# The last four steps' expert results summed on chip, and a place of its own for the first expert's w1 in the second layer

## Chip, cores and metric

The kernel runs on one core of one Trainium2 chip. The metric is the device time of one execution in microseconds; three executions of the kernel before took 1209.22 to 1213.81 us, median 1212.03. All data are fp32.

## What is computed

Two layers over 256 image rows (x) and 256 context rows (ctx) of 1024 columns. Each layer: modulation, one input projection cut into five groups (Fourier mix, differential attention, gated unit), output projection, residual and layer norm. Then comes the part that matters here, a mixture of 16 experts of which each row uses 2:

```python
def _moe(h, gates, w1, w3, w2):
    y = jnp.zeros_like(h)
    for e in range(N_EXPERTS):                       # 16
        a = jax.nn.silu(h @ w1[e]) * (h @ w3[e])     # 1024 -> 512
        y = y + gates[..., e:e + 1].astype(h.dtype) * (a @ w2[e])
    return y

    hx = _modulate(x, sh2, sc2)
    yx = _moe(hx, _route(hx, w_router, router_bias), moe_w1[l], moe_w3[l], moe_w2[l])
    x = _layernorm(DEEPNORM_ALPHA * x + g2 * yx, ln_g[l, 1], ln_b[l, 1])
    # ctx likewise, in the first layer only
```

`_route` gives each row two experts with weights that sum to 1. The experts' three matrices are 2 MB each, 6 MB an expert, 96 MB a layer.

## The kernel before

It is written engine by engine, with semaphores; each engine runs its own program in order. Rows stand in tiles of 128: T = 4 tiles in layer 0 (2 of x, 2 of ctx), T = 2 in layer 1. PSUM has 8 banks; `plan_layer` hands them out job by job (`claim`, `full`, `freed`, `read`), and an `("at", b)` skips to bank b.

**Experts as steps.** Rows are sorted by expert into blocks of 32 (`ROWS`). Each block is a step; an expert has one step or more, and their number is known only at run time (`META`, written by DVE after routing: counts, steps before each expert, steps in all). The trace shows 41 steps in layer 0, five of them the first expert's, and 25 in layer 1, one of them the first expert's. Per step: PE `turn_rows` (transposes), `up` (w1 and w3, 32 matmuls of 128x256 in four column groups, L1781), `turn_act` (L1789), `down` (w2, 16 matmuls, L1797); DVE `copy_up`, `rows_out`, `product`, `copy_out`; ACT stages the rows and computes the silu. `beside(n)` is work that DVE does in steps 0 to 2: the weights `WK2` of each row's two experts and the residual of each tile, scaled by the first norm's vectors.

**Rows through DRAM.** POOL's queue scatters the modulated rows into `xg_rows` by destination (`DEST`), loads 32 rows per step, and stores each step's results in `y_rows` (`store_rows`, four DMAs, from the double buffer `YO`). The first three steps take their rows from PE instead (`collect`). When all steps are stored and all stores have landed, POOL gathers for each tile t two rows per row (`indirect_dma_start`, L718) into `G2`, two tiles at a time; ACT weighs one (`weigh`, L790), DVE adds the other, multiplies by the gate and adds to X (`mix`), takes statistics, and POOL computes the root (`rstd`, L650). Then DVE normalises. In layer 1 the result goes to the output by two DMAs of ACT's queue.

**Expert weights.** SP's queue loads them into a ring of three experts: slots 0 to 2 and 3 to 5 of W, and three tensors lent by the rest of the layer (RAB, XT, H). The first loads of a layer are written out (`for s in (0, 2, 1, 3)`, L558 to L570), each waiting for the last reader of its place; H comes when the scatter has landed. `follow(e, p)` loads expert e once expert e-3 has been used, w1 and w3 after its `up`, w2 after its `down`. After the loop the next layer's input projection is loaded; the chunk f waits for all gathers.

**From layer 0 to layer 1.** PE turns each normalised tile (`hT`), ACT modulates it (`modulated`, L777), PE projects (L1542). Before that, ACT runs `lambdas(1)` (an exponential for the attention) and DVE `lam(1)`, which computes its input and waits for its result.

## Time and profile before

| | |
|---|---|
| median of three runs | 1212.03 us (1209.22 to 1213.81) |
| profiled execution | 1212.09 us |
| its span, first to last instruction | 1210.4 us |
| PE busy | 989.6 us, 82% |
| DVE, ACT, POOL busy | 326.3, 226.4, 257.2 us |
| mean granted clock of TensorE | 0.922 |
| moved by DMA | 331.4 MB, mean 274 GB/s |
| chain that ended last | PE 71%, DMA 13%, issue 8%, DVE 4% |

"PE" is TensorE's matmuls, "PEld" its weight loads, "DVE" VectorE, "ACT" ScalarE, "POOL" GpSimd, "SPq" the queue of DMA issues. An fp32 matmul shows as two records (passes). A row's last bracket tells how long the engine was idle before it and what ended that. "issue" is time in which nothing that the profile shows was waited for.

### The profile page before, as it was taken

The numbers are of one execution on the slowest core, as the hardware profiler recorded it, in microseconds if no ns is written. First come the engines' busy times: TensorE is split into PE (matmuls) and PEld (weight loads), VectorE is DVE, ScalarE is ACT, GpSimd is POOL, SyncE is SP. The second block draws the span as 40 slices with busy tenths as digits, with TensorE's granted clock in tenths as the row PEclk, the third lists the DMA queues.
The fourth block names the chain that finished last, engine by engine and source line by source line (L and its number), as shares of the span: only waits on it lengthen the run. The fifth ranks groups of instructions, "written<-read, shape, count | busy, mean of one in ns | idle before, by whom it ended". The sixth has DMA issues, their size and how long they took to land.

```text
span 1210.4 us, 24004 instructions
## 1 busy us (share of the span) xinstructions
PE 989.6 (82%) x9029; PEld 555.9 (46%) x9030; DVE 326.3 (27%) x766; ACT 226.4 (19%) x556; POOL 257.2 (21%) x483
## 2 busy tenths in 40 slices
PE   3999999999999889988886449998988768747860
PEld 1444645564665545544543224635555334423430
DVE  1003033633345222212211166105324312111115
ACT  1311112740231111101100133104412001000100
POOL 0200000010035434433331320000101314321431
PEclk9999999989899999999997869999998879978995
DMA  9994475390365784589999956527665999999942
GB/s 338 368 410 198 157 261 209 139 368 14 139 237 160 285 313 168 183 343 361 394 393 398 372 169 221 180 99 278 271 250 220 400 398 395 395 407 410 390 156 104
DMA packets 89109, 331.42 MB, mean 274 GB/s; under 512 B 10780, under 2 KB 13036, under 8 KB 64484
## 3 DMA queue, kind: packets, MB, share of 16 engines
q1 hardware_dynamic: 66500, 282.13, 60.7%
q0 software_dynamic: 21088, 47.48, 11.1%
q10 hardware_dynamic: 1472, 1.12, 0.3%
q8 instruction: 34, 0.56, 0.2%
q14 instruction: 15, 0.12, 0.0%
HBM read 303.18 MB, written 27.53 MB: 273 GB/s over the span
## 4 chain that ended last, share of the span: by engine, by line
PE 71%; DMA 13%; issue 8%; DVE 4%; ACT 1%; SPq 1%; POOL 1%; POOLq 0%; DVEq 0%; ACTq 0%
PE PS L1781 18%; PE PS L1542 16%; PE PS L1797 8%; PE PS L1704 7%; DMA W<-in_moe_w 5%; DMA XT<-in_moe_w 5%; PE PS L1475 3%; PE PS L1771 3%; PE PS L1508 3%; PE PS L1558 3%; PE PS L1789 2%; DMA W<-in_w_ada 2%; PE PS L1666 1%; PE PS L1654 1%; PE PS L1751 1%
## 5 line engine op out<-in xcount | busy, mean ns | idle before, releaser
L1781 PE MATMUL PS<-W,EX 128*32 128x256 f32 x2944 | 180.5, 398 | 48.0 <-issue 26.3
L1542 PE MATMUL PS<-W,XT 128*128 128x512 f32 (+1 forms) x480 | 189.1, 554 | 2.4 <-ACT XT L777 2.4
L1781 PEld LDWEIGHTS PS<-W,EX 128*32 128x32 f32 x2944 | 97.6, 114 | 116.7 <-issue 64.3
L1542 PEld LDWEIGHTS PS<-W,XT 128*128 128x128 f32 x480 | 91.1, 191 | 95.6 <-issue 93.2
L752 ACT ACTIVATE AT<-EX 64x512 f32<-64x512 f32 x64 | 40.4, 631 | 399.0 <-PE PS L1771 387.6
L650 POOL TENSOR_TENSOR RSTD<-VAR,HALF 128x1 f32<-128x1 f32 (+1 forms) x24 | 16.3, 683 | 457.7 <-DVE VAR L1056 457.7
L1781 PE MATMUL PS<-RAB,EX 128*32 128x256 f32 x640 | 83.2, 419 | 33.3 <-DMA XT<-in_moe_w 19.9
L1346 DVE COPY EX<-PS 128x256 f32<-128x256 f32 x66 | 28.0, 424 | 292.8 <-PE PS L1781 292.8
L681 POOL DMA_DIRECT2D y_rows<-AT x136 | 67.5, 497 | 174.7 <-DVE AT L1356 165.0
L1797 PE MATMUL PS<-W,AT 128*32 128x256 f32 x1472 | 95.1, 402 | 1.5 <-DVE AT L1353 1.5
L681 POOL DMA_DIRECT2D y_rows<-EX x128 | 63.5, 496 | 153.0 <-DVE EX L1356 138.9
L1704 PE MATMUL PS<-W,XT 128*128 128x512 f32 x192 | 83.1, 593 | 0.0
L1781 PE MATMUL PS<-XT,EX 128*32 128x256 f32 x640 | 83.1, 419 | 0.0
L677 POOL DMA_DIRECT2D EX<-xg_rows x136 | 67.8, 500 | 53.2 <-issue 37.0
L1771 PE MATMUL PS<-C,AT 64*128 64x64 f32 x272 | 46.0, 289 | 31.7 <-issue 31.6
L1781 PEld LDWEIGHTS PS<-RAB,EX 128*32 128x32 f32 x640 | 39.5, 120 | 67.0 <-issue 46.2
L1771 PEld LDWEIGHTS PS<-C,AT 64*128 64x128 f32 x272 | 37.6, 209 | 61.8 <-issue 61.8
L777 ACT ACTIVATE XT<-PS,MB,MA 128x128 f32<-128x128 f32 x112 | 40.6, 470 | 128.6 <-PE PS L1508 128.6
L1797 PEld LDWEIGHTS PS<-W,AT 128*32 128x32 f32 x1472 | 45.1, 114 | 30.9 <-issue 6.2
L1704 PEld LDWEIGHTS PS<-W,XT 128*128 128x128 f32 x192 | 36.2, 190 | 44.0 <-issue 44.0
L1349 DVE COPY EX<-PS 128x256 f32<-128x256 f32 x68 | 28.9, 424 | 54.1 <-PE PS L1771 54.1
L1508 PE MATMUL PS<-C,X 128*128 128x128 f32 x112 | 16.6, 298 | 32.2 <-DVE X L1075 32.2
(202 smaller groups left out, 1059.4 us busy)
## 6 DMA issues: line engine op xcount, KB each, us to landing
W<-in_moe_w SPq DMA_DIRECT2D x66, 2048.0 KB, 19.6
W<-in_w_ada SPq DMA_DIRECT2D x24, 2048.0 KB, 11.0
RAB<-in_moe_w SPq DMA_DIRECT2D x10, 2048.0 KB, 21.1
XT<-in_moe_w SPq DMA_DIRECT2D x10, 2048.0 KB
H<-in_moe_w SPq DMA_DIRECT2D x10, 2048.0 KB, 17.7
W<-in_w_in SPq DMA_DIRECT2D x7, 2048.0 KB, 21.2
EX<-xg_rows POOLq DMA_DIRECT2D x136, 64.0 KB, 5.7
W<-in_w_out SPq DMA_DIRECT2D x4, 2048.0 KB, 18.8
```

Of the source, the lines that this page charges most:

```text
L677: pool.dma_start(XRAW[b][ROWS * q:ROWS * q + ROWS, :], part_of_rows(xg_rows, n, slice(512 * q, 512 * q + 512))) .then_inc(rows_in[b][L], 16)
L681: pool.dma_start(part_of_rows(y_rows, n, slice(256 * q, 256 * q + 256)), YO[b][ROWS * q:ROWS * q + ROWS, :]) .then_inc(y_written[b][L], 16)
L752: nc.scalar.activation(dst, src, ACT.Copy).then_inc(done, 1)
L777: ins = nc.scalar.activation(XT[:, n, P * t:P * t + P], ps[:, P * k:P * k + P], ACT.Identity, bias=MB[:, kind, n, t // 2:t // 2 + 1], scal ...
L1475: pe.matmul(ps[32 * n:32 * n + 32, :], CT[:, k, :], w[n][:, k, :], start=(k == 0), stop=False, tile_position=(0, 32 * n))
L1508: mm = pe.transpose(ps[:, P * n:P * n + P], piece, IDENT)
L1542: mm = pe.matmul(ps[:, 0:cw], XT[:, k, P * t:P * t + P], w[:, k, :], start=(k == 0), stop=(k == KD - 1))
L1558: mm = pe.matmul(ps, XT[:, k, P * t:P * t + P], w[:, k, :], start=(k == 0), stop=(k == KD - 1))
L1704: mm = pe.matmul(ps, XT[:, k, P * t:P * t + P], w[:, k, :], start=(k == 0), stop=(k == KD - 1))
L1771: mm = pe.transpose(ROWS_PS[:, 2 * ROWS * k:2 * ROWS * k + 2 * ROWS], turned[:, k, :], IDENT[0:2 * ROWS, 0:2 * ROWS])
L1781: mm = pe.matmul(UP_PS[o:o + ROWS, 0:256], rows, moe_up(p, n)[:, k, 256 * a:256 * a + 256], start=(k == 0), stop=(k == KD - 1), tile_posit ...
L1797: mm = pe.matmul(DOWN_PS[o:o + ROWS, 0:256], rows, moe_down(p)[:, k, 256 * q:256 * q + 256], start=(k == 0), stop=(k == FE // P - 1), tile ...
```

## The change

1. POOL still stores each step's results in DRAM, but the rows of the last four steps are not read from there. `YO` becomes a ring of four (in `R4`). Stores stop two steps earlier. The gathers are issued when the third last step has been copied out (whose copy waited for the landing of the fifth last step's store) and the places for `G2` are free: RAB for tiles 0 and 1, H for 2 and 3. Rows in the last four steps get destination 0 and weight 0 there (`DESTE`, `WE`).
2. PE sums. `combine(t)` adds, for each quarter of the columns in a bank of its own, the gathered rows times diagonal matrices of the weights (`DIAG`, made by ACT), and the last four steps' results (in `YO`) times a selection matrix `OHT`, 32 rows high, in four row groups. `shares()` (DVE, in `beside(0)`) makes the early flags and the matrices `OH`; PE turns them after the first expert (job `oht`), ACT copies them to SBUF after the loop.
3. ACT's `weigh` goes; `mix` on DVE multiplies PSUM by the gate and adds to X. In layer 1 the gate is applied earlier: `copy_out` multiplies by `GQ` instead of copying (one PE job `gq` in place of `spread`), X is added by PE with the identity, and `finish` takes statistics and normalises straight from PSUM.
4. Layer 0: `lam(1)` moves behind the four mixes on DVE, `load_ln(0, 1)` on POOL behind the last combine; the residual of tile 0 moves from `beside(0)` to `beside(1)`.
5. Layer 1: w1 of expert 0 is loaded to half of H and to X's tiles 2 and 3, as soon as the last hT is turned. Slot 0 takes expert 3's w1 instead. The load to H (expert 2's w2) waits for expert 0's `up`.

```diff
@@ SP
+            def first_w1():
+                full(sp, ("hT", DEPTH - 1, 3, 1))
+                src = moe_w1[DEPTH - 1, 0, :, :].rearrange("(q p k) n -> q p k n", q=2, p=P)
+                for q in range(2):
+                    sp.dma_start(FIRST_W1[q], src[q, :, :, :]).then_inc(first_w1_in, 16)
-                    for s in (0, 2, 1, 3):
+                    for s in (0, 2, 1, 3) if L + 1 < DEPTH else (2, 1, 3, 0):
                         full(sp, last[s])
-                        moe_load(L, s // 3, s % 3, s // 3)
+                        moe_load(L, s // 3, s % 3, s // 3 if s or L + 1 < DEPTH else RING3)
...
+                    sp.wait_ge(meta_ready, L + 1)
+                    if L + 1 == DEPTH:
+                        sp.wait_ge(up_done[L], steps_before(sp, L, 1))
                     moe_load(L, 2, 2, 2)
...
+                if key == ("in", DEPTH - 1, "v"):
+                    first_w1()
@@ POOL
-                        with pool.If(total > n):
+                        with pool.If(total > n + 2):
...
+                pool.wait_ge(S["early_ready"], val("early_ready", L, 0))
+                wait_apart(pool, out_copied[L], pool.value_load(META[0:1, L, 0, NEXP:NEXP + 1], min_val=1, max_val=BLOCKS - 1))
+                through = steps_before(pool, L, NEXP - 1)
+                wait_apart(pool, up_done[L], through)
+                for t in range(T):
+                    if t == 2:
+                        wait_apart(pool, down_done[L], through)
+                    for k in range(2):
+                        pool.indirect_dma_start(out=G2[t][:, k, :], out_offset=None, in_=y_rows[0:BLOCKS * ROWS, :],
+                                                in_offset=bass.IndirectOffsetOnAxis(ap=DESTE[:, t, k:k + 1], axis=0))\
+                            .then_inc(g_in[t], 16)
...
+                if L + 1 < DEPTH:
+                    full(pool, ("cb", L, T - 1, 3))
+                    load_ln(L, 1)
@@ ACT
+                act.wait_ge(S["early_ready"], val("early_ready", L, 0))
+                for t in range(T):
+                    for k in range(2):
+                        ins = nc.scalar.activation(DIAG[t // 2][:, t % 2, k, :], IDENT, ACT.Copy, scale=WE[:, k, t:t + 1])
+                ins.then_inc(S["diag_ready"], 1)
...
+                act.wait_ge(S["affine"], val("affine", L, 0))
+                for t in range(T):
+                    key = ("oht", L, t)
+                    copy(OHT[L][:, t, :, :].rearrange("p b n -> p (b n)"), full(act, key), freed(key))
                 if L + 1 < DEPTH:
                     lambdas(L + 1)
@@ DVE
+                def shares():
+                    early, first = GS[:, 0:2, 0:T], PM[:, 0, :]
+                    link(dve.tensor_scalar(T1[:, 0, :], CNT[:, 3, 16:17], float(ROWS), -4.0 * ROWS, ALU.mult, ALU.add))
+                    link(dve.tensor_scalar(early, DF[:, :, 0:T], T1[:, 0, :], None, ALU.is_lt))
+                    dve.tensor_tensor(WE[:, :, 0:T], WK2[:, 0:T, :].rearrange("p t k -> p k t"), early, ALU.mult)
...
+                    for t in range(T):
+                        second = (WKS, OHS)[t % 2][:, :, :, :].rearrange("p k t e -> p (k t e)")
+                        for k, place in enumerate((OH[t], second)):
+                            ins = dve.tensor_scalar(place, rows, DF[:, k, t:t + 1], WK2[:, t, k:k + 1], ALU.is_equal, ALU.mult)
+                        link(ins)
+                        dve.tensor_tensor(OH[t], OH[t], second, ALU.add).then_inc(S["late_ready"], 1)
...
+                def mix(t):
+                    g0 = G2[t][:, 0, :]
+                    let_go(dve.tensor_tensor(by_quarter(g0), combined(t), by_quarter(GT[:, t // 2, :]), ALU.mult), t)
+                    link(dve.tensor_tensor(X[:, t, :], X[:, t, :], g0, ALU.add))
+                    stats(L, "ln2", t)
+                    normalise(L, "ln2", t, S["ln2_norm"])
...
+                for t in range(T):
+                    mix(t) if L + 1 < DEPTH else finish(t)
+                if L + 1 < DEPTH:
                     lam(L + 1)
@@ PE
+                for t in range(T):
+                    pe.wait_ge(S["late_ready"], val("late_ready", L, t))
+                    ps, done = claim(("oht", L, t))
+                    for b in range(4):
+                        for q in range(4):
+                            mm = pe.matmul(ps[ROWS * q:ROWS * q + ROWS, P * b:P * b + P], OH[t][:, ROWS * b:ROWS * b + ROWS],
+                                           IDENT, start=True, stop=True, tile_position=(0, ROWS * q))
+                    mm.then_inc(done, 1)
...
+                def combine(t):
+                    g_wait(pe, L, t)
+                    banks = [claim(("cb", L, t, q)) for q in range(4)]
+                    for q, (ps, _) in enumerate(banks):
+                        cs = slice(256 * q, 256 * q + 256)
+                        if L + 1 == DEPTH:
+                            pe.matmul(ps[:, 0:256], IDENT, X[:, t, cs], start=True, stop=False)
+                        for k in range(2):
+                            pe.matmul(ps[:, 0:256], DIAG[t // 2][:, t % 2, k, :], G2[t][:, k, cs],
+                                      start=(L + 1 < DEPTH and k == 0), stop=False)
+                    if t == 0:
+                        wait_apart(pe, out_copied[L], total + 1)
+                    read(pe, ("oht", L, t))
+                    for b in range(4):
+                        for q, (ps, done) in enumerate(banks):
+                            mm = pe.matmul(ps[:, 0:256], OHT[L][ROWS * q:ROWS * q + ROWS, t, b, :],
+                                           YO[ROWS * q:ROWS * q + ROWS, b, :], start=False, stop=(b == 3),
+                                           tile_position=(ROWS * q, 0))
...
+                for t in range(T):
+                    combine(t)
```

## Rows read from the trace of the kernel before

**Rows 1.** The page, 40 slices of the span: busy tenths of DMA.
```profile
DMA  9994475390365784589999956527665999999942
```
**Rows 2.** Busy time by windows (columns as in the row above it), and PE's waits, 340 to 700.
```profile
core 0: us, PE busy (x) PEld busy (x) DVE busy (x) ACT busy (x) POOL busy (x), PEclk, DMA share, GB/s
580.00:590.00 10.00, 8.96 (x138) 5.05 (x137) 2.71 (x7) 1.82 (x4) 3.06 (x7) 1.00 1.02 401
...
PE PS L1781 <- DMA XT<-in_moe_w: 8.4, 1, 8.4
```
**Rows 3.** Chain that ended last, end of layer 0: start, duration, what.
```profile
627.67 28.59 DMA XT<-in_moe_w
...
714.31 8.84 PE PS L1542 x16
...
724.02 6.87 PE PS L1542 x16
```
**Rows 4.** Busy time by windows, layer 1.
```profile
750.00:760.00 10.00, 10.00 (x25) 4.42 (x24) 3.85 (x4) 0.60 (x1) 0.00 (x0) 1.00 0.01 2
...
1000.00:1020.00 20.00, 17.62 (x274) 10.10 (x262) 4.24 (x11) 2.49 (x6) 8.00 (x17) 1.00 1.02 395
```
**Rows 5.** Chain, the last landing that PE waited for.
```profile
1070.10 34.81 DMA W<-in_moe_w
```
**Rows 6.** Engines in order of time, first steps of layer 0.
```profile
343.28 0.29 DVE L1312 TENSOR_TENSOR AB<-C,DF 128x128 f32<-128x128 f32 x1
...
364.33 1.23 DVE L1081 SCALAR_TENSOR_TENSOR X<-X,KT 128x1024 f32<-128x1024 f32 x1
...
366.73 0.42 DVE L1346 COPY EX<-PS 128x256 f32<-128x256 f32 x1
...
367.85 0.51 PE L1789 MATMUL PS<-C,EX 128*128 128x128 f32 x2
```
**Rows 7.** Engines in order of time, end of layer 0 and start of layer 1.
```profile
673.21 2.27 POOL L681 DMA_DIRECT2D y_rows<-AT  x4 [2.91 <-DVE AT L1356]
...
681.91 1.93 PE L1797 MATMUL PS<-W,AT 128*32 128x256 f32 x32 [0.74 <-DVE AT L1353]
...
687.15 0.20 ACT L784 ACTIVATE LAM<-LAM 128x2 f32<-128x2 f32 x1 [3.09 <-DVE LAM L997]
...
703.97 1.22 DVE L1417 TENSOR_TENSOR H<-H,RC 128x1024 f32<-128x1024 f32 x1
...
706.49 1.28 DVE L1060 BATCH_NORM_STATS2 ST<-X 128x6 f32<-128x512 f32 x2
...
708.90 0.81 DVE L1075 TENSOR_SCALAR X<-X,MV,RSTD 128x1024 f32<-128x1024 f32 x1 [0.70 <-POOL RSTD L650]
...
711.16 2.90 ACT L777 ACTIVATE XT<-PS,MB,MA 128x128 f32<-128x128 f32 x8 [4.85 <-PE PS L1508]
```
**Rows 8.** Engines in order of time, end of layer 1.
```profile
1163.02 2.27 POOL L681 DMA_DIRECT2D y_rows<-AT  x4 [2.85 <-DVE AT L1356]
...
1171.64 1.93 PE L1797 MATMUL PS<-W,AT 128*32 128x256 f32 x32 [0.74 <-DVE AT L1353]
...
1181.52 1.00 POOL L718 DMA_INDIRECT H<-y_rows,DEST  x1 [3.38 <-issue]
...
1188.18 1.15 ACT L790 ACTIVATE H<-H,WK 128x1024 f32<-128x1024 f32 x1 [16.97 <-DMA H<-y_rows,DEST]
...
1205.79 1.28 DVE L1072 SCALAR_TENSOR_TENSOR X<-X,RSTD,KT 128x1024 f32<-128x1024 f32 x1
```
**Rows 9.** Chain (128x256 matmuls), then PE and its weight loads, two row groups.
```profile
181.06 3.45 PE PS L1616 x16
...
204.70 0.30 PEld L1654 LDWEIGHTS PS<-KT,H 64*128 64x128 f32 x4
204.70 1.99 PE L1654 MATMUL PS<-KT,H 64*128 64x512 f32 x8
```
**Rows 10.** Chain and SP's queue, first steps of layer 1.
```profile
928.79 0.64 PE PS L1771 x4
...
929.73 0.37 SPq L539 DMA_DIRECT2D H<-in_moe_w  x1
...
937.79 4.80 issue
```

More of the change, by code:

```diff
@@ L450, in g_wait @@
         def g_wait(eng, L, t):
-            eng.wait_ge(g_in[t % 2], 32 * (sum(tiles(l) for l in range(L)) // 2 + t // 2 + 1))
+            eng.wait_ge(g_in[t], 32 * sum(tiles(l) > t for l in range(L + 1)))
         def wait_apart(eng, semaphore, value):
@@ L596, in _ @@
                 if key == ("in", key[1], "f") and key[1]:
[L598 to L599 removed]
+                    for t in range(4):
+                        g_wait(sp, key[1] - 1, t)
                 rows = slice(0, KD)
```

210 lines of the change are left out of this document (124 added, 86 removed).

## Prediction

> **What bounds the kernel now.** I read the page first, then the busy shares in windows, then the chain that ended last, and last the engines in order of time around the four places that the diff touches. No one engine bounds the run: PE is busy for 82% of it, and the slices of DMA reach 9 in two long stretches, the end of each layer's expert loop [rows 1]. In layer 0 the expert loop is PE's for its first 200 us: in the whole loop PE waits once for a weight, 8.4 us, and only from about 550 us do the windows show DMA full (1.02) [rows 2]. That one wait is the landing at 656.3 us of a load issued at 627.67 [rows 3]. In layer 1 the windows show the DMA share at 1.02 from 935 to 1155 us while PE is idle for a tenth or more [rows 4], and the chain goes through landings up to 1104.9 us [rows 5]; the ten steps after it are PE's alone. So a 2 MB weight load moved out of that stretch is worth its transfer time, and a microsecond of PE at its start is worth nothing. Between the loops (714 to 925 us) and after them only latency counts: the last result must be stored, read back by the gathers, weighed, added, normalised.
>
> **Layer 0, first expert: +6.9 us.** Three things are added beside step 0. DVE computes the shares (7 small operations, then 3 of 128x128 for each of 4 tiles) in place of one residual (2 x 1.23). Small ones took about 0.2 and a 128x128 one 0.29 [rows 6], so 1.4 + 4 x 0.76 = 4.4 against 2.5: +1.9. After the old residual, DVE copied `up` out at 366.73 and was done 0.7 before PE turned it at 367.85 [rows 6]; 1.2 are left over, 1.3 with the late waits. The residual that leaves goes to step 1, where a double residual already fitted without moving PE. ACT's 8 diagonal copies lie in its idle time (it waits 5 us and more per step); uncovered they would cost 2.4. PE gets 4 x 16 matmuls with 32 weight columns and 128 moving ones, after the first expert's five steps, where PE is what everybody waits for. No row has this form. At the pace of `down` (32 passes in 1.9 us with 256 columns [rows 7]) one tile takes 1.9; with half the columns, if nothing but columns counted, 0.95. I take 1.4, the middle, because weight loads and issue are not halved: 5.6. Ends for the whole part: 4.7 and 9.3. PE is the trigger of the loads, and the DMA stretch that ends in the 8.4 us wait begins at 550 us with loads that PE releases; so it starts later by as much, and I pass all of it on.
>
> **Layer 0 to layer 1: +7.0 us.** Before, `down` ended at 683.84 [rows 7] and the first projection began at 714.31 [rows 3]; stores, landing, gather, weighing and the first normalisation lie between. Now:
> - The gathers start when step total-3 is copied and stored: the store at 673.21 took 2.27 [rows 7], the way from a last store to the first gather 3.38 [rows 8], so 678.9. A pair lands 6.7 after its start (1181.52 to 1188.18 [rows 8]). Here the next layer's weights fill the DMA, and I add 1.2: 686.8, that is 3 us after PE is free. The other pairs follow at 2.5 us or, if the weight stream halves their rate, 5.2; either way the last is there before PE wants it at about 703.
> - `combine(t)` is 8 matmuls of 128x256 at 0.43 (16 passes in 3.45 us [rows 9]), 3.4, and 16 of 32x256 in four row groups. Two row groups ran together: 8 passes of 512 columns took 1.99 us, one after another they would be 3.4; and 4 weight loads in two groups took 0.30, the start of the second pair included [rows 9]. Four groups at once give 1.75, plus start 1.9. So 5.3 a tile, and 1.5 for a clock that falls in the 3 us of idleness (the cold first projection took 8.84, the next one 6.87 [rows 3]; 2.0 is the upper bound): first tile at 693.6.
> - DVE mixes four tiles: multiply 1.25, add 1.25, statistics 1.3, the small ones, POOL's root and the scaling 2.0 [rows 7], together 5.8, one operation less than before. That is longer than PE's 5.3, so DVE sets the pace: 693.6 + 23.2 = 716.8.
> - The decisive point is a wait. `lam(1)` now stands behind all four mixes on DVE, and ACT's `lambdas(1)` waits for it; before, both were done by 687.4 in the shadow of the stores [rows 7]. Queued behind it on ACT is the modulation of the very first tile, and the first projection behind that. 1.0 for lam's four small operations at 0.25, 0.25 for the exponential, 2.9 for the modulation [rows 7], 0.3 of handovers: 721.3 against 714.31. PE has by then idled 10 us, so its projection is as cold as before and the old 8.84 stays.
>
> Ends: +3.5 (gathers unslowed, no clock loss) and +10 (a slower multiply out of PSUM, late gathers). `load_ln` for layer 0 is moved behind the last combine on POOL, with `load_sgu_w` behind it; both land by about 730, and are read after 750.
>
> **The first w1 of layer 1: -4.8 us.** It is loaded after the last hT, near 745 us, where the DMA is empty (share 0.01 from 750 to 760 [rows 4]). The ada loads queued behind it on SP are wanted 50 us later. Slot 0 then takes expert 3's w1 with the loads at 856, again outside the full stretch. In the stretch one load fewer is moved: 2.1 MB at 395 GB/s [rows 4] is 5.3. Against it stands the load into H, which on SP must now wait for the first expert's `up`: that ended at 928.8, and H was issued at 929.73, when the scatter had landed [rows 10], so only a register load of 0.4 is added; behind it are expert 3's loads. Step 0 of this layer gets shares and oht too, which makes `down(0)` 2 us later; w2 of expert 3 waits for it on SP, with two loads still in flight: nothing. Between -5.3 and -2.0. The gate row in place of the spread takes 3 us off PE ahead of `collect`, of which none counts, since H waits for the scatter.
>
> **The end: -12.5 us.** Stored at 1163.02 + 2.27, first gather 3.4 later, 6.66 to land: 1175.35, against the end of the last `down` at 1173.57 [rows 8]. A tile has 12 matmuls of 0.43 and the 16 narrow ones: 7.1. So tile 0 at 1182.45, tile 1 at 1189.55. `finish` is 1.4 + 0.4 + 1.3 + 1.3 = 4.5 by the old durations, and after the last operation at 1207.07 the output took 3.3 to the end of the span [rows 8]: 1197.4, 13.0 early; 0.5 off for the clock. Ends -15 and -9. POOL, copying, and the multiply by the gate in `copy_out` stay hidden.
>
> **Two rules of the skill.** The trace shows pairs of row groups together, never four. The Trainium skill, "TensorE: Matmul & The Clock Gate", Part 3, gives 3.07x for four row tiles of 512 columns, not 4x; by it the narrow part is 2.2 a tile and the end 0.6 later. Against the change speaks "TensorEngine Tiling (Array Packing)", PSUM Bottleneck, in the Trainium skill: after packing, emptying PSUM may become the limit. The rows agree, as DVE's 5.8 exceeds PE's 5.3.
>
> **Sum.** 6.9 + 7.0 - 4.8 - 12.5 = -3.4. The profiled execution took 1212.09 us for a span of 1210.4, and the median of the runs is 1212.03, the same: 1208.6. All low ends together give -12, all high ends +8.
>
> **Rivals.**
> 1. The layer-0 additions are swallowed by the 8.4 us wait. It would need loads that PE's delay doesn't move; the full stretch from 550 us speaks for it, the partly idle DMA just before against. Then -10.3: 1201.8. Chance 0.18.
> 2. ACT's wait for lam isn't what comes last, and the modulation starts when PE has turned tile 0 at about 710. Then the transition is -3: 1198.4. The program's order speaks against it. 0.08.
> 3. The early w1 brings nothing, because the stretch has another pace, such as ring slots that PE frees: +1.4: 1213.4. Against it the share of 1.02. 0.10.
> 4. The slower side: four row groups don't run together. Then 16 x 0.43 = 6.8 in place of 1.9. In layer 0 the combines set the pace, 10.2 each: the last at 729.5, the projection at 740; in layer 1 twice 4.9. Together +25 on my sum: 1237. It decides from about 3.5 us a tile, where the total turns positive. The two-group rows speak against it. 0.09.
>
> My forecast keeps 0.55. A measurement here can tell 0.5% (6 us) from no change. Faster by more: rivals 1 and 2 nearly whole and a fifth of the forecast, 0.35. Slower: rival 4, and the far ends of 3 and the forecast, 0.12. The rest, 0.53, is the same. The range of 1199 to 1218 leaves out rival 4 and the last ends.
>
> **What would show it.** Right: the first projection of layer 1 some 14 us later than 714 (6.9 + 7.0), ACT's exponential after the fourth mix, no DMA gap from 935 on, about 24 us from the last `down` to the end instead of 37. Wrong: an oht tile far from 1.4 us, narrow matmuls starting one after another, the expert loop of layer 0 ending where it did, or PE standing on instructions of the new code (4.8 us of "issue" stand at 937.8 already [rows 10]).

## The result and the profile after

The changed kernel takes 1222.71 us (median of 6 runs, 1220.43 to 1226.41) against 1212.99 for the kernel before beside it (6 runs, 1209.22 to 1215.11): ratio 1.0089, 95% interval 1.0072 to 1.0107. It is 0.9% slower. The forecast was 1208.6 with a range of 1199 to 1218. The profiled execution has a span of 1221.1 us against 1210.4.

To see where the 10.7 us went, both spans are cut at the same events, all read from the engines in order of time: DVE's copies of `up` (`copy_up`, one per step, 41 in layer 0 and 25 in layer 1) and the start of layer 1's first projection q0. "After, again" (e6_again, the changed kernel once more) and e13_layer1_only are experiments that are explained below.

| stretch, us | before | after | after, again | e13 |
|---|---|---|---|---|
| start to the first copy_up | 359.8 | 362.8 | 359.1 | 361.0 |
| layer 0: first to last copy_up | 317.5 | 325.8 | 324.5 | 315.2 |
| last copy_up to q0 | 37.0 | 46.5 | 46.5 | 37.0 |
| q0 to layer 1's first copy_up | 214.6 | 218.3 | 217.8 | 217.7 |
| layer 1: first to last copy_up | 238.2 | 236.7 | 238.6 | 234.6 |
| last copy_up to the end | 43.3 | 31.0 | 31.0 | 31.1 |
| span | 1210.4 | 1221.1 | 1217.5 | 1196.6 |

The first stretch holds nothing of the change and moved by 3.7 us between two executions of one kernel, so a microsecond or two of any single difference is scatter. The end is worth what was forecast. The other places came out worse than forecast: by 1.4, 2.5, 3.7 and 3.3 us from layer 0's loop to layer 1's in the profile after, and by 0.1, 2.5, 3.2 and 5.2 in the second.

The page's two rows of 40 slices (the clock that PE was granted, and the busy tenths of DMA; the latter answers [rows 1]):

```profile
PEclk9899999989899999999997988999997999978999
DMA  9995475380363685669999971735585699999972
```

**Layer 0, first expert.** DVE, then PE, in order of time (start, us, engine, line, operation, out <- in, idle before and who ended it); they answer [rows 6]:

```profile
367.31 0.15 DVE L1363 TENSOR_SCALAR T<-CNT 128x1 f32<-128x1 f32 x1
...
371.82 0.29 DVE L1378 TENSOR_TENSOR EX<-EX,OHS 128x128 f32<-128x128 f32 x1
372.04 0.41 DVE L1400 COPY EX<-PS 128x256 f32<-128x256 f32 x1
...
372.50 0.50 PE L1886 MATMUL PS<-C,EX 128*128 128x128 f32 x2 [1.60 <-DVE EX L1400]
375.30 5.35 PE L1879 MATMUL PS<-W,EX 128*32 128x256 f32 x64 [2.30 <-issue]
```

`shares()` runs from 367.31 to 372.1, 4.8 us, about what was worked out (4.4). But the copy of `up` that stood 0.7 us before PE wanted it is now at 372.04, PE waits 1.60 and then 2.30 more with nothing that the profile shows, and the next `up` runs at the lower clock (0.72 granted from 375 to 381 us): 5.35 us, where the others take 3.66. Most of the 2.30 isn't new. The kernel before has 1.66 at the same place, with the `up` behind it at full clock:

```profile
370.01 3.66 PE L1781 MATMUL PS<-W,EX 128*32 128x256 f32 x64 [1.66 <-issue]
```

So the late copy costs 1.6 of waiting, 0.6 of issue and 1.7 of clock, together 3.9 of the 4.0 us by which the third copy_up comes later behind the first than before.

The turns of the selection matrices (`oht`) on PE:

```profile
400.98 1.94 PE L1966 MATMUL PS<-C,AT 128*32 128x128 f32 x64
...
404.16 1.52 PE L1966 MATMUL PS<-C,EX 128*32 128x128 f32 x48 [0.81 <-issue]
407.50 0.67 PE L1868 MATMUL PS<-C,AT 64*128 64x64 f32 x4 [1.83 <-issue]
```

Four tiles and a gap of 0.81 take 400.98 to 405.7, and 1.83 of issue follow (1.18 in the kernel before). Two tiles take 1.94, so one takes 0.97 and not the 1.4 of the prediction; the gaps make up the rest.

**Layer 0 to layer 1.** PE, DVE and ACT, answering [rows 3] and [rows 7]:

```profile
693.20 1.93 PE L1894 MATMUL PS<-W,AT 128*32 128x256 f32 x32 [0.74 <-DVE AT L1407]
699.38 5.38 PE L1988 MATMUL PS<-RAB,AB 128*128 128x256 f32 x16 [4.25 <-DMA RAB<-y_rows,DESTE]
704.69 2.01 PE L1995 MATMUL PS<-R,KT 32*128 32x256 f32 x32
706.63 3.72 PE L1988 MATMUL PS<-RAB,AB 128*128 128x256 f32 x16
...
723.40 1.09 PE L1596 MATMUL PS<-C,X 128*128 128x128 f32 x8
735.07 10.04 PE L1630 MATMUL PS<-W,XT 128*128 128x512 f32 x16 [10.58 <-ACT XT L817]
...
707.08 1.22 DVE L1488 TENSOR_TENSOR RAB<-PS,RC 128x1024 f32<-128x1024 f32 x1 [11.27 <-PE PS L1995]
...
713.06 1.22 DVE L1488 TENSOR_TENSOR RAB<-PS,RC 128x1024 f32<-128x1024 f32 x1
...
730.80 0.22 DVE L1035 TENSOR_TENSOR JUNK<-LM 128x64 f32<-128x64 f32 x1
...
731.82 0.20 ACT L824 ACTIVATE LAM<-LAM 128x2 f32<-128x2 f32 x1 [34.67 <-DVE LAM L1036]
731.93 2.89 ACT L817 ACTIVATE XT<-PS,MB,MA 128x128 f32<-128x128 f32 x8
```

PE waits 4.25 us for the first gathered rows, its 16 weighted passes take 5.38 in place of 3.72 because the clock has fallen, and the 32 narrow passes take 2.01. Then DVE sets the pace (707.08, 713.06, ...: 5.9 a tile), while PE starts a tile every 5.6 and has summed the last at 723.4. `lam(1)` comes behind the fourth mix (730.80), ACT's exponential behind that, the modulation of tile 0 behind that, and q0 at 735.07. ACT's row for the exponential shows an idle time of 34.67 us, ended by DVE's LAM.

**Layer 1, first experts.** PE ahead of `collect` and in the second `up`, and busy time by windows (us, then PE, PEld, DVE, ACT, POOL busy, granted clock, DMA share, GB/s), answering [rows 4] and [rows 10]:

```profile
938.70 0.38 PE L1829 MATMUL PS<-GATE,C 128*128 128x16 f32 x2
939.01 1.08 PE L1838 MATMUL PS<-C,GATC 128*32 128x128 f32 x16
941.74 5.62 PE L1848 MATMUL PS<-H,AB 128*32 128x512 f32 x16 [1.65 <-DVE AB L1346]
...
954.51 1.07 PE L1879 MATMUL PS<-W,EX 128*32 128x256 f32 x16 [0.17 <-DVE EX L1403]
960.33 4.02 PE L1879 MATMUL PS<-W,EX 128*32 128x256 f32 x48 [4.75 <-issue]
...
core 0: us, PE busy (x) PEld busy (x) DVE busy (x) ACT busy (x) POOL busy (x), PEclk, DMA share, GB/s
960.00:965.00 5.00, 4.67 (x80) 3.14 (x83) 0.92 (x3) 0.00 (x0) 0.00 (x0) 0.71 1.01 392
965.00:970.00 5.00, 3.26 (x78) 2.31 (x68) 0.42 (x1) 0.63 (x1) 0.00 (x0) 1.00 0.22 92
970.00:975.00 5.00, 3.84 (x66) 2.23 (x62) 3.07 (x4) 0.28 (x1) 2.94 (x6) 1.00 0.61 231
```

The gate row takes 1.08 us where the spread took 3.66. PE then stands for 1.65 and `collect` runs cold, 5.62 in place of 3.63. The 4.8 us of issue at 937.79 [rows 10] are there again, 4.75 at 955.58, but now inside the second `up`, behind its first 16 passes, instead of behind the first `down`; the 48 passes that follow take 4.02, where the same number took 2.80 in layer 0 at full clock. `down(0)` starts 15.0 us after the first copy_up (968.43 against 953.4); with the kernel before it was 6.5. The w2 load of expert 3 waits for it on SP, and the DMA share falls to 0.22 and 0.61: the queue stood idle for some 6 of these 10 us.

**The end.** PE and DVE, answering [rows 8]:

```profile
1194.68 1.93 PE L1894 MATMUL PS<-W,AT 128*32 128x256 f32 x32 [0.74 <-DVE AT L1407]
1198.31 0.67 PE L1986 MATMUL PS<-X,C 128*128 128x256 f32 x2 [1.70 <-DMA RAB<-y_rows,DESTE]
...
1203.65 2.01 PE L1995 MATMUL PS<-R,X 32*128 32x256 f32 x32
...
1205.94 1.43 DVE L1497 BATCH_NORM_STATS2 ST<-PS 128x6 f32<-128x256 f32 x4 [8.65 <-PE PS L1995]
...
1213.26 1.42 DVE L1497 BATCH_NORM_STATS2 ST<-PS 128x6 f32<-128x256 f32 x4 [2.58 <-PE PS L1995]
...
1216.71 1.28 DVE L1506 SCALAR_TENSOR_TENSOR X<-X,RSTD,KT 128x1024 f32<-128x1024 f32 x1 [0.35 <-DVE X L1503]
```

First gathered rows 1.70 us behind the last `down`, 7.3 us a tile, and 24.5 us from the last `down` to the end of the span, against 36.8.

### The profile page after: what moved, and what is told of

Read it like the earlier page. It is cut to its first block, busy times and chain, and to the rows that moved or that the text cites. A ratio compares the mean times of both kernels' runs of the same rounds, so it can differ in the third digit from the quotient of the medians.

```text
span 1221.1 us, 24955 instructions
## 1 busy us (share of the span) xinstructions
PE 1037.9 (85%) x9525; PEld 591.5 (48%) x9526; DVE 320.8 (26%) x792; ACT 226.1 (19%) x567; POOL 245.5 (20%) x459
## 3 DMA queue, kind: packets, MB, share of 16 engines
q0 software_dynamic: 20320, 46.43, 10.6%
## 4 chain that ended last, share of the span: by engine, by line
PE 71%; DMA 13%; issue 7%; DVE 5%; ACT 1%; SPq 1%; POOL 1%; POOLq 0%; DVEq 0%; ACTq 0%
PE PS L1879 17%; PE PS L1630 15%; DMA W<-in_moe_w 8%; PE PS L1894 8%; PE PS L1792 7%; PE PS L1563 3%; PE PS L1868 3%; PE PS L1596 3%; PE PS L1646 3%; DMA XT<-in_moe_w 2%; PE PS L1886 2%; DMA W<-in_w_ada 2%; PE PS L1848 1%; PE PS L1742 1%; PE PS L1754 1%
## 5 line engine op out<-in xcount | busy, mean ns | idle before, releaser
L1879 PE MATMUL PS<-W,EX 128*32 128x256 f32 x2912 | 185.4, 406 | 53.7 <-issue 32.3
L1630 PE MATMUL PS<-W,XT 128*128 128x512 f32 (+1 forms) x480 | 190.3, 557 | 10.6 <-ACT XT L817 10.6
L713 POOL DMA_DIRECT2D y_rows<-R x248 | 123.0, 497 | 327.0 <-DVE R L1411 166.3
L1879 PE MATMUL PS<-RAB,EX 128*32 128x256 f32 x640 | 80.6, 409 | 26.8 <-DMA XT<-in_moe_w 17.1
L1894 PE MATMUL PS<-W,AT 128*32 128x256 f32 x1472 | 91.1, 389 | 1.5 <-DVE AT L1407 1.5
L1879 PE MATMUL PS<-XT,EX 128*32 128x256 f32 x640 | 80.5, 409 | 0.0
L709 POOL DMA_DIRECT2D EX<-xg_rows x128 | 63.9, 500 | 49.1 <-issue 32.7
L1894 PE MATMUL PS<-H,AT 128*32 128x256 f32 x640 | 38.7, 382 | 0.0
L1879 PEld LDWEIGHTS PS<-XT,EX 128*32 128x32 f32 x640 | 38.0, 118 | 0.0
```

What stands on the lines that cost most here:

```text
L709: pool.dma_start(XRAW[b][ROWS * q:ROWS * q + ROWS, :], part_of_rows(xg_rows, n, slice(512 * q, 512 * q + 512))) .then_inc(rows_in[b][L], 16)
L713: pool.dma_start(part_of_rows(y_rows, n, slice(256 * q, 256 * q + 256)), YO[ROWS * q:ROWS * q + ROWS, b, :])\
L1630: mm = pe.matmul(ps[:, 0:cw], XT[:, k, P * t:P * t + P], w[:, k, :], start=(k == 0), stop=(k == KD - 1))
L1879: mm = pe.matmul(UP_PS[o:o + ROWS, 0:256], rows, w[:, 256 * a:256 * a + 256], start=(k == 0), stop=(k == KD - 1), tile_position=(0, o))
L1894: mm = pe.matmul(DOWN_PS[o:o + ROWS, 0:256], rows, moe_down(p)[:, k, 256 * q:256 * q + 256], start=(k == 0), stop=(k == FE // P - 1), tile ...
```

## The experiments

Each row of the table has the median, the ratio to the kernel before on the same chip with its 95% interval, and the stretches of the table above from one profile: loop of layer 0, transition (trans., last copy_up to q0), q0 to the first copy_up (att., where the attention lies), loop of layer 1, tail.

| run | median | ratio | loop 0 | trans. | att. | loop 1 | tail |
|---|---|---|---|---|---|---|---|
| e1_lam_early | 1216.01 | 1.0056 (1.0034-1.0077) | 324.3 | 37.4 | 217.0 | 238.4 | 35.1 |
| e2_old_w1 | 1222.3 | 1.0114 (1.0066-1.0161) | 323.7 | 44.8 | 215.4 | 240.0 | 34.3 |
| e3_oht_late | 1224.49 | 1.0114 (1.0089-1.0138) | 319.6 | 50.2 | 217.9 | 234.9 | 38.0 |
| e4_w1_alone | 1206.35 | 0.9957 (0.9937-0.9977) | 315.8 | 36.9 | 216.1 | 233.0 | 43.2 |
| e5_late | 1209.89 | 0.9999 (0.9983-1.0014) | 315.6 | 42.4 | 215.4 | 235.0 | 37.6 |
| e6_again | 1221.85 | 1.0090 (1.0057-1.0123) | 324.5 | 46.5 | 217.8 | 238.6 | 31.0 |
| e7_no_gather | 1202.81 | 0.9937 (0.9918-0.9956) | 325.0 | 33.1 | 214.6 | 240.8 | 29.2 |
| e8_shares_late | 1221.55 | 1.0090 (1.0056-1.0124) | 315.8 | 50.2 | 218.0 | 235.2 | 37.4 |
| e9_combined | 1206.0 | 0.9955 (0.9936-0.9973) | 317.5 | 42.3 | 218.4 | 235.2 | 31.1 |
| e10_w1_again | 1207.26 | 0.9957 (0.9937-0.9978) | 315.9 | 37.3 | 214.7 | 232.9 | 43.2 |
| e11_lam_again | 1216.38 | one run | 326.2 | 38.9 | 215.3 | 238.9 | 33.0 |
| e12_w1_turns | 1207.41 | 0.9973 (0.9951-0.9996) | 313.9 | 37.0 | 216.0 | 232.9 | 43.6 |
| e13_layer1_only | 1195.27 | 0.9851 (0.9827-0.9876) | 315.2 | 37.0 | 217.7 | 234.6 | 31.1 |
| e14_layer1_late | 1197.39 | 0.9864 (0.9842-0.9886) | 317.4 | 37.1 | 215.8 | 231.9 | 31.1 |

**e1_lam_early.** The wait that the prediction called decisive, taken away alone.

```diff
+                    lam(L + 1)
                     for c_ in (10, 11):
 ...
                 for t in range(T):
                     mix(t) if L + 1 < DEPTH else finish(t)
-                if L + 1 < DEPTH:
-                    lam(L + 1)
```

> The changed kernel with one edit: on DVE lam(1) runs before the four mixes of layer 0, as it did in the kernel before. Theory (a wait behind the mixes): in the changed kernel the first modulation of layer 1 starts only after the fourth mix and lam, 7 us after PE has turned the first tile. With lam early, ACT modulates tile 0 right after PE's transpose, the first projection starts 7 us sooner after the last down of layer 0, and the time is 1222.7 - 7 = 1216. Rival (the combines and the gathers set the pace, the wait is only what the chain happens to name): less than 2 us change, 1221 to 1223.

Faster than the changed kernel, by 6.7 us between the medians and by 4.0 between the two ratios (1.0056, 1.0089), whose intervals just touch. ACT, then PE:

```profile
700.11 0.20 ACT L824 ACTIVATE LAM<-LAM 128x2 f32<-128x2 f32 x1 [5.38 <-DVE LAM L1036]
717.51 2.90 ACT L817 ACTIVATE XT<-PS,MB,MA 128x128 f32<-128x128 f32 x8 [17.20 <-PE PS L1595]
...
720.66 8.80 PE L1629 MATMUL PS<-W,XT 128*128 128x512 f32 x16 [2.81 <-ACT XT L817]
```

The exponential is done at 700.1 and the modulation now waits only for PE's turn of tile 0, 17 us later. q0 starts 37.4 us after the last copy_up instead of 46.5, 9.1 earlier, and the transition is as long as with the kernel before. Two other pairs of kernels that differ in this edit show 7.6 (the changed kernel and e11_lam_again, whose transition is 38.9) and 7.8 (e8_shares_late and e5_late). So 7.6 to 9.1 of the +9.5 hung on this wait. The tail gives 4.1 of it back, by idle times that are told of at the end.

**e2_old_w1.** The early w1 undone in the changed kernel (slot order, `first_w1`, the fill counts back as before).

> The changed kernel with the early load of the first expert's w1 undone: layer 1's weights are loaded in the order of the kernel before. Theory (the early load's gain is lost, because the DMA queue now runs dry for 6 us early in layer 1 while w2 of expert 3 waits on SP for the late first down): with one more load in the queue at that point it does not run dry, so undoing costs only about 1 us: 1224. Rival (the early load gives its 5 us and something else in layer 1 costs as much): undoing costs 5 us, 1227.5.

1222.3, no more than the changed kernel itself. The time can't settle it: the interval of this ratio is 0.5% wide to either side, 6 us, which leaves room for no gain and for one of 5. The stretch tells more: layer 1's loop is 240.0 without the early w1 and 236.7 to 238.9 with it (the changed kernel twice, e1_lam_early, e11_lam_again). So some 1 to 3 us of its 5 are left, by one profile without it.

**e4_w1_alone.** The same edit the other way round: the kernel before with the early w1 and nothing else.

> The kernel before with only the early load of the first expert's w1 (own place, slot 0 takes expert 3's w1, the load to H waits for the first up). Theory (the load leaves a stretch in which the DMA is full, and the first down is not late here): -4.8 against before, 1208. Rival (with one load fewer in flight the queue runs dry in front of expert 3's w2 in any case): 0 to -1, 1212 to 1213.

Held: ratio 0.9957, -5 us, loop of layer 1 5.2 us shorter (238.2 to 233.0), and e10_w1_again gave the same in another batch. The term of -4.8 was right for the kernel it was worked out from. It doesn't add to the rest of the change.

**e3_oht_late.** The 16 matmuls a tile of `oht` moved on PE from behind the first expert to behind the last `down`.

> The changed kernel with PE's turning of the selection matrices (job oht) moved from behind the first expert to behind the last down of each layer, where PE waits for the gathers. Theory: 5.2 us of PE come out of layer 0's loop and cost 1 us at its end, since PE idles 4.3 us there; in layer 1 the first down comes 4 us sooner, the DMA idles 4 us less, and the end pays 1 to 2 us: in all -4 - 3 = -7, 1215.5. Rival (the 4.8 us of issue before the second up is what makes the DMA run dry, not the turning): layer 1 gives nothing, -4 and +1.5: 1220.

A miss: both loops got shorter (5 to 6 and 2 to 4 us), and the time didn't. The transition grew by 3.7 and the tail by 7.0. Work taken out of the first expert came back behind the loop, where nothing hides it.

**e5_late, e8_shares_late, e6_again, e7_no_gather** ran on one chip.

> e3_oht_late with the selection matrices also made behind DVE's loop and residual(0) beside step 0 again (e5_late without the early lam). Against e3_oht_late it prices DVE's share of the first expert: the prediction put it at 1.3 us in layer 0 and nothing in layer 1, the changed kernel's trace shows about 4 us in layer 0 (copy_up late, then an up at the lower clock). Theory: layer 0's loop is about 2 to 4 us shorter than the 319.6 us of e3_oht_late, layer 1's 0 to 2 us, and the time 1219 to 1221; against e5_late it is some 7 us longer. Rival (the 1.3 us of the prediction): 1223.

Against e3_oht_late the loop of layer 0 is 3.8 us shorter (315.8) and that of layer 1 the same (235.2 and 234.9). So DVE's share of the first expert costs 3.8 in layer 0, not 1.3, and nothing in layer 1. Together with the turns (e6_again to e3_oht_late: 4.9) layer 0's first expert costs 8.7 from the level of e8_shares_late. The six profiles that have this loop as before (the kernel before, e4, e10, e12, e13, e14) give 313.9 to 317.5, mean 316.0, and the six that have it as changed (the changed kernel twice, e1, e2, e7, e11) 323.7 to 326.2, mean 324.9: 9.0 apart. And the tail shows why moving it doesn't pay; DVE, then PE:

```profile
1189.05 0.17 DVE L1371 TENSOR_SCALAR PM<-T 128x4 f32<-128x4 f32 x1 [1.61 <-issue]
...
1191.18 0.29 DVE L1381 TENSOR_TENSOR AT<-AT,OHS 128x128 f32<-128x128 f32 x1
...
1184.83 1.93 PE L1898 MATMUL PS<-W,AT 128*32 128x256 f32 x32 [0.74 <-DVE AT L1410]
1190.68 3.21 PE L1979 MATMUL PS<-C,AT 128*32 128x128 f32 x64 [3.92 <-DVE AT L1381]
1194.92 0.67 PE L1990 MATMUL PS<-X,C 128*128 128x256 f32 x2 [1.03 <-ACT X L792]
```

The last `down` ends at 1186.8. DVE starts on the matrices at 1189.05, PE waits 3.92 for them, turns them with the clock down (3.21), waits 1.03 for ACT's copies, and its first weighted pass comes at 1194.92: 8.2 us behind the last `down`, where the changed kernel had 1.70.

> The changed kernel with three edits: lam(1) ahead of the mixes, the oht matmuls on PE behind the last down (as in e3_oht_late), and of shares() only the four instructions that POOL and ACT need stay beside step 0, while the selection matrices OH are made on DVE behind its loop, under the wait for the gathers; residual(0) is beside step 0 again as in the kernel before. Theory (the work put in the first expert of each layer is what the change pays for, and it starves the weight queue in layer 1): layer 0's loop goes back to about 318 us from first to last copy_up (325.8), layer 1's to about 234 (236.7), the transition is that of e1_lam_early (37.4), the tail 31 to 35; with -7, -7, -3 and 0 to +4 against the changed kernel's 1222.7 this gives 1206 to 1210, and 1202 if the tail stays at 31. Rival (work taken out of the first expert only comes back behind the loop, as e3_oht_late gained nothing): 1216, the time of e1_lam_early.

1209.89, the time of the kernel before, with the edits of e8_shares_late and e1_lam_early together. The time and the loops (315.6 and 235.0) came out as expected, the ends didn't: the transition is 42.4 and not 37.4, the tail 37.6 and not 31 to 35, both for the reason shown in the rows above. Against e8_shares_late on the same chip the early lam is worth 11.7 us, more than the 7 expected; 7.8 of it are in the transition and 2.6 between q0 and the first copy_up.

> The changed kernel unaltered, for a second profile beside the others. In e1_lam_early, e2_old_w1 and e3_oht_late ACT's gate and DVE's copy_out sat idle for 4.4 to 5.9 us behind the last down while POOL issued the gathers, and in the changed kernel's own profile they did not. Theory (these idle times vary by execution): the time is again 1222 to 1223, and the profile may show them at either end, with a tail of 34 to 35 us instead of 31.0. Rival (they belong to the edits of those three kernels): the profile shows none, and a tail of 31.

The changed kernel again: 1.0090, the same ratio in another batch, none of the idle times, tail 31.0.

> e1_lam_early with its indirect gathers left out: POOL only counts up the semaphores on which PE, ACT and DVE wait, so that the gathered rows are whatever lay in those buffers (that part of the sum is left out). Theory (the idle times of 4.4 to 5.9 us on ACT and DVE behind the last down come from the gathers being issued): they are gone from both ends, and PE's first combination no longer waits for a landing (4.25 us in layer 0, 1.70 in layer 1 in the changed kernel), so the tail is 28 to 30 us instead of 35.1, the transition some 32 to 34 instead of 37.4, and the time 1205 to 1208 against 1216. Rival (the idle times have another origin): tail 33 or more, and the time 1210 to 1213.

Without gathers 1202.81, a ratio lower by 0.012 than that of e1_lam_early, some 14 us. The two ends account for 10.2 of the two spans' 10.6: 4.3 in the transition, 5.9 in the tail (of which 4 are the idle times below). It isn't a clean comparison. What PE sums here isn't the rows, so layer 1 routes other rows: its loop has 26 steps instead of 25, and 240.8 us holds one step more. The two ends are what compares: against e11_lam_again, the same kernel as e1_lam_early without the idle times, they are shorter by 9.6 us (5.8 and 3.8). More than that isn't to be had there from faster gathers.

**e9_combined, e10_w1_again, e11_lam_again, e12_w1_turns** ran on one chip. e9_combined has the early lam, makes the matrices beside step 0 in layer 1 and behind the loop in layer 0, and turns them behind the last `down` in banks that the first combination doesn't use (in layer 0 those of tiles 2 and 3 within that combination):

```diff
-    for t in range(T):
-        jobs += [("at", (7 + 2 * t) % 8), ("oht", L, t)]
     jobs += [("moe", L)]
+    for t in range(T):
+        jobs += [("at", 5 + 2 * (t % 2)), ("oht", L, t)]
```

> The changed kernel rearranged by what the runs so far showed: lam(1) ahead of the mixes; in layer 0 the selection matrices OH made behind DVE's loop, in layer 1 beside step 0 (where e8_shares_late showed no price); the oht matmuls behind the last down in banks 5 and 7, so that combine(0) in banks 0 to 3 doesn't wait for ACT's copies of them (in e8_shares_late PE waited for OH until 3.9 us behind the last down, took 3.2 us for the turns and 1.0 for the copies, 6.4 us more tail than the changed kernel's 31.0). Theory: against e5_late the loops stay (315.6 and 235.0 us), the transition goes from 42.4 to 38 and the tail from 37.6 to 31 or 32, 10 us in all: ratio to the kernel before 0.992, some 1201 us. Rival (the turns behind the last down cost what they cost wherever their bank is): 1207, ratio 0.997.

Half a miss. The tail is 31.1, 6.5 better than in e5_late: in layer 1 the turns fit under the wait for the gathers. The transition stays at 42.3. DVE, then PE, in layer 0:

```profile
686.89 0.17 DVE L1374 TENSOR_SCALAR PM<-T 128x4 f32<-128x4 f32 x1 [1.61 <-issue]
...
690.90 0.29 DVE L1384 TENSOR_TENSOR EX<-EX,OHS 128x128 f32<-128x128 f32 x1
...
682.67 1.93 PE L1900 MATMUL PS<-W,AT 128*32 128x256 f32 x32 [0.74 <-DVE AT L1413]
688.73 3.44 PE L1982 MATMUL PS<-C,AT 128*32 128x128 f32 x64 [4.13 <-DVE AT L1384]
692.10 3.86 PE L1998 MATMUL PS<-RAB,AB 128*128 128x256 f32 x16
```

Four tiles of matrices take DVE until 691.2, PE stands for 4.13 and turns the first two tiles' cold. The whole comes to 1206.0, no better than the early w1 alone:

> The kernel before with the early w1 alone, as in e4_w1_alone, for a comparison with e9_combined on one chip. Theory: ratio 0.9957 to the kernel before again, some 4 us slower than e9_combined. Rival: e9_combined's sum on chip brings nothing and both have the same time.

0.9955 and 0.9957: its rival held. All of the sum on chip, well placed, brought nothing over e10_w1_again, since what it saves at the end (12.1 us) it pays in layer 0 (1.6 in the loop, 5.0 in the transition), in layer 1's loop (2.3) and before it (3.7).

> e1_lam_early again, one look. Its first profile had idle times of 4.4 to 5.9 us on ACT and DVE behind the last down, which e5_late, e6_again and e8_shares_late didn't show. Theory (they belong to the chip or the execution, not to the kernel): they are absent here, and the tail is 31 us instead of 35.1. Rival (they belong to this kernel): they are here again.

The idle times are absent, so this kernel doesn't always have them; the tail is 33.0 and not 31, since the clock fell during its first combination (0.66 granted from 1190 to 1195 us).

> The kernel before with the early w1 (e10_w1_again) and in layer 1 alone the oht matmuls of the changed kernel at their place behind the first expert, on constants and with nobody reading them. Theory (PE's work and the gap behind it hold back down(0), and with it the load of the next w2, so that the weight queue runs dry and the early w1's gain goes): layer 1's loop takes 236 to 238 us from first to last copy_up instead of the 233.1 of e4_w1_alone, and the time is 3 to 4 us above e10_w1_again. Rival (the queue has slack enough): at most 1 us above.

A miss that teaches. The turns stand at the changed kernel's place, on constants:

```profile
930.50 1.94 PE L1892 MATMUL PS<-C 128*32 128x128 f32 x64
934.18 0.66 PE L1794 MATMUL PS<-C,AT 64*128 64x64 f32 x4 [1.75 <-issue]
934.77 1.93 PE L1820 MATMUL PS<-W,AT 128*32 128x256 f32 x32
```

They take 1.94 and some 1.75 of issue behind them. Layer 1's loop is 232.9, exactly that of e10_w1_again, and the DMA share stays at 1.00 to 1.03 from 930 to 945 us. The turns alone don't starve the weight queue. What the changed kernel has and this one hasn't is the 4.75 of issue inside the second `up`. But neither has this one the 4.7 of issue that e10_w1_again has behind `down(0)`, so its loop isn't a clean price of the turns either.

**e13_layer1_only.** Layer 0 as before (all steps stored, gathered, weighed on ACT and added on DVE, with lam(1) ahead), the change in layer 1 alone. Its core:

```diff
-    for t in range(T):
+    for t in range(T if L + 1 == DEPTH else 0):
         jobs += [("at", (7 + 2 * t) % 8), ("oht", L, t)]
 ...
-                        with pool.If(total > n + 2):
+                        with pool.If(total > n + 2 * (L + 1 == DEPTH)):
 ...
-                        shares()
+                        if L + 1 == DEPTH:
+                            shares()
```

> The change in layer 1 alone: layer 0 sums by gathering all rows of all steps, weighing on ACT and adding on DVE, as the kernel before does (its gathers have four buffers now), with lam(1) ahead of the mixes; layer 1 keeps the early w1, the sum on chip and the four steps' results in YO, as changed. Theory (layer 0's part is what makes the change slow: from its first copy_up to the start of q0 the kernel before takes 354.5 us, e4_w1_alone 352.7, e1_lam_early 361.7, e9_combined 359.8, while layer 1's part saves 12.3 us at the end): that stretch takes 353 to 355 us, layer 1's loop about 238 (as in e6_again and e11_lam_again, with its oht matmuls where the change has them), the tail 31; the time 1199 to 1203, ratio 0.991 to 0.994. Rival (the gain at the end is eaten in layer 1's own loop and layer 0 was no cause): 1206 or more, no better than e4_w1_alone.

1195.27, ratio 0.9851: 1.5% faster than the kernel before, and better than the 1199 to 1203 expected. The early w1 is in it, which alone gives 0.9957 (e4_w1_alone, e10_w1_again), so the sum on chip in layer 1 adds some 1.1%. Against the changed kernel's profile 20.1 of the 24.5 us lie in layer 0's loop and transition, 2.1 in layer 1's loop, 1.8 in the first stretch, which no edit touches. Its first experts in layer 1, on PE:

```profile
932.13 3.66 PE L1902 MATMUL PS<-W,EX 128*32 128x256 f32 x64 [0.20 <-DVE EX L1423]
937.34 2.16 PE L1989 MATMUL PS<-C,AT 128*32 128x128 f32 x64 [1.55 <-DVE AT L1397]
941.10 0.67 PE L1891 MATMUL PS<-C,AT 64*128 64x64 f32 x4 [1.60 <-issue]
941.70 1.94 PE L1917 MATMUL PS<-W,AT 128*32 128x256 f32 x32
```

PE waits for the matrices (1.55), yet the 4.75 us of issue stand nowhere here, `down(0)` comes 10.75 us after the first copy_up instead of 15.0, and the loop takes 234.6. So the matrices' wait isn't what costs most there, as I had expected of e14_layer1_late.

**e14_layer1_late.** e13_layer1_only with layer 1's turns behind the last `down`.

> e13_layer1_only with layer 1's oht matmuls behind the last down, in banks 5 and 7, as e9_combined has them. e12_w1_turns ran the same matmuls at the early place on constants and lost nothing (loop of layer 1 232.9 us), so the matmuls themselves aren't what delays down(0) there. Theory (PE's wait for the selection matrices, which DVE makes late, is what costs 3 to 5 us at the early place): the third copy_up of layer 1 comes 19.0 us behind the first instead of 22 to 24.5, the loop takes 235 us instead of 238, the tail stays at 31; 3 us below e13_layer1_only: 1196 to 1200. Rival: the early place costs nothing by the end of the loop, the weight queue sets the pace, and both have the same time.

The rival held: 0.9864 against 0.9851, intervals that overlap. In the profile the loop is 2.7 shorter, but its third copy_up comes 20.5 us behind the first (19.8 in e13_layer1_only), not 19.0; 4.75 of issue are back, behind `down(0)` as in the kernel before. In the time the place of the turns in layer 1 makes no difference that can be measured.

Put side by side, the loops of layer 1 with the early w1 fall into groups by two things. With the 4.4 to 5.2 us of issue behind `down(0)` or absent, and no early turns that wait for their matrices (e4_w1_alone, e10_w1_again, e12_w1_turns, e14_layer1_late): 231.9 to 233.0. Turns on real matrices but no such gap (e13_layer1_only): 234.6. The gap inside the second `up`, without turns (e3_oht_late, e5_late, e8_shares_late, e9_combined): 234.9 to 235.2. Both (the changed kernel twice, e1_lam_early, e11_lam_again): 236.7 to 238.9.

## Why the prediction was wrong

By the steps of its sum (forecast -3.4, measured +9.7 between the medians, +10.7 and +7.1 between the two profiles and that before). Of the 14.1 and 10.5 us between forecast and profile, 3.3 and 5.2 lie in layer 1's loop, 3.7 and 3.2 ahead of it, 2.5 and 2.5 in the transition, 1.4 and 0.1 in layer 0's loop, and 3.0 and -0.7 in the first stretch, where nothing was changed:

- **The end, -12.5: right.** -12.3 in the profile, and in each later kernel that has it (tail 31.0 to 31.1 where nothing disturbed it). Four row groups run together: 32 narrow passes in 2.01 us (forecast 1.9), a tile in 7.3 (7.1). Rival 4 is out. (Its "+25 on my sum" is the change against the kernel before; on the sum it is +28.5, which gives its 1237.) The estimate by the Trainium skill's 3.07x ("TensorE: Matmul & The Clock Gate", Part 3) was 2.2; the row of 2.01 stands between the two.
- **Layer 0, first expert, +6.9: the total nearly right (+7.0 and +8.3 in two profiles, 9.0 between the means of six and six), in part by luck.** The oht term was 5.6 and is 4.9 to 6.2 (either profile of the changed kernel against e3_oht_late), but a tile took 0.97 and not 1.4, which the prediction named as a sign of being wrong; gaps of 0.81 and of 0.65 more than before fill the term up. DVE's part was 1.3 and is 3.8. The slack was read nearly right (PE waits 1.60); the step that failed is that the working stopped there and put what follows such a wait at nothing, 0.6 of issue and 1.7 of clock (5.35 in place of 3.66). Rival 1 (swallowed by the 8.4 us wait) is out: the landing moved from 656.3 to 667.1 with the rest.
- **Layer 0 to layer 1, +7.0: mechanism right, size 2.5 short (+9.5).** The first combination started 4.25 behind the last `down`, not 3.0 (the first pair of gathers landed 9.5 us after its start, not 7.9), it was 0.5 longer, the handover to DVE took 0.4, and the mixes went at 5.93 a tile, not 5.8: 0.5 more. Three pairs of kernels show that 7.6 to 9.1 of the 9.5 hung on the wait for `lam(1)`. Rival 2's condition, brought about in e1_lam_early, gives the old length (37.4 against 37.0) and not 3 us less than it, as the rival forecast, since PE turns tile 0 only behind its fourth combination. The PSUM rule of the Trainium skill ("TensorEngine Tiling (Array Packing)", PSUM Bottleneck) held as cited: DVE at 5.9 a tile, PE at 5.6.
- **q0 to the first expert: forecast 0, is +3.7 and +3.2.** Part of it may be scatter: kernels that differ in nothing give 216.1 and 214.7 (e4_w1_alone, e10_w1_again), and 217.0 and 215.3 (e1_lam_early, e11_lam_again). In the first profile 1.2 is a q0 colder than before (10.04 against 8.84), and 1.3 lies between the projections and the second layer's output matmuls, in both profiles of the changed kernel, and I found no cause in the change; 1.2 is `collect`. The prediction said of the 3 us that the gate row saves that "none counts". In fact less work ahead of a wait made it worse: PE stood and came back cold.
- **The early w1, -4.8: right alone, mostly lost in combination.** e4_w1_alone and e10_w1_again show -5. In the changed kernel layer 1's loop gained 1.5, or lost 0.4 in the second profile. By e2_old_w1 the other edits cost this loop 1.8 (240.0 against 238.2), which the sum put at nothing, and the early w1 then gives back 1.1 to 3.3 and not 4.8. The step that failed: "which makes `down(0)` 2 us later; ... with two loads still in flight: nothing". `down(0)` came 8.5 later than before relative to the first copy_up, and the DMA share fell to 0.22. Of that, 6.0 is the issue gap that moved into the second `up`, with the lower clock behind it, and 2.6 the turns and their gap. The gap stood in [rows 10] and was named as a risk, but not priced: nothing was asked about what would follow if it fell on the other side of `down(0)`. That the late `down(0)` is what cost the loop its gain is read from the traces; no run moved it alone.
- **Rival 3** (1213.4, early w1 worth nothing) came nearest; its condition (another pace of the stretch) isn't what happened, since alone the edit works.

The sum's terms were each taken for the kernel before with one edit. Several met in PE's first experts, where there was 0.7 us of slack, and made each other worse.

What stays open: what places the 4.4 to 5.2 us of issue in layer 1's first steps. They stand inside the second `up` in every kernel whose layer 0 sums on chip, behind `down(0)` in the kernel before, e4_w1_alone, e10_w1_again and e14_layer1_late, and not there in e12_w1_turns and e13_layer1_only, where gaps of 2.14 and 1.88 follow and one of 3.9 at 966 and 973 us. They move with the code around them; no run here tells by what rule. The traces hold a lead: in the changed kernel, the kernel before and each experiment that has the gap, exactly one packet of the queue that the page calls "q8 instruction" (16 KB) moves within it, and so it is in the two of 3.9. Other packets of this queue move without a gap of that length, and that PE stood for one isn't shown. The tie to the loop's length is seen across kernels, and no run moved the gap alone.

## What to carry over

A term worked out for one edit holds for that edit alone: e4_w1_alone gave its 5 us, and by the loops the same edit gave 1 to 3 once other edits stood around it. Before adding work at the start of a loop that paces a transfer queue, add up everything that reaches the first instruction on which that queue waits, with the gap and the fallen clock that can follow a wait of PE. And weigh a scheme place by place: summing on chip was worth 12 us where the run ends and nothing followed, cost 17 to 20 in layer 0's loop and transition, where four tiles and a next layer's start stood around it, and used only in the first place, with the early w1, it beats both kernels (0.9851).

## What the runs showed of the hardware

- **A wait of PE can cost more than its length, but not each does.** In the rows above 1.60 of waiting brought 0.6 more of issue and 1.7 of lower clock; 1.65 brought 2.0 (`collect` in 5.62); 4.25 brought 1.7. But 1.55 in e13_layer1_only brought 0.2 (turns in 2.16 in place of 1.94), and the 1.70 at the end of the changed kernel brought nothing: the granted clock is 1.00 from 1198 to 1206 us.
- **Idle times without a visible cause.** In the profiles of e1_lam_early, e2_old_w1 and e3_oht_late, taken on one chip, DVE and ACT sat idle at both loop ends while POOL issued its gathers, e.g. in layer 1 of e1_lam_early (DVE, then PE):

```profile
1183.17 0.42 DVE L1413 TENSOR_TENSOR R<-PS,RC 128x256 f32<-128x256 f32 x1 [5.22 <-remote]
1183.51 0.28 DVE L1407 TENSOR_TENSOR AT<-PS,EX 128x128 f32<-128x128 f32 x1
...
1183.89 3.64 PE L1893 MATMUL PS<-W,AT 128*32 128x256 f32 x32 [4.10 <-DVE AT L1407]
```

The `down` that DVE waited for had ended at 1179.35, 3.8 us earlier; the profile names no instruction for the release, only "remote". It cost the tail 4 us (35.1 against 31.0). e5_late, e6_again, e8_shares_late, e9_combined and e11_lam_again (the same kernel as e1_lam_early, in another batch) show none. So it seems to vary by chip or execution; which, and why beside gathers, isn't known.
- **Landing of one gather, in the chains:** 5.1 to 5.5 us in the kernel before (both layers) and in e13_layer1_only, 8.2 and 8.3 in layer 0 of the changed kernel and of e11_lam_again; in the changed kernel the windows show a DMA share of 1.04 from 690 to 700 us. With e13_layer1_only's gathers of the same layer it was 0.83 from 695 to 700.
